# Down weights of a routed expert as two neighbouring rows for each partition, hidden features split into even and odd

## The reference

```
D_MODEL, SEQ, N_EXPERTS, TOP_K, EXPERT_DIM = 1024, 512, 64, 8, 256

def swiglu(t, wg, wu, wd):
    return (jax.nn.silu(t @ wg) * (t @ wu)) @ wd

# moe_ffn: every token goes to 8 of 64 experts, chosen by sigmoid scores
#   w_e_gate, w_e_up: (64, 1024, 256)      w_e_down: (64, 256, 1024)
    yb = swiglu(xb, w_e_gate[e], w_e_up[e], w_e_down[e])
    return yb * wb[:, None]
    ...
shared = swiglu(t, w_sh_gate, w_sh_up, w_sh_down)     # one expert for all tokens
```

## Time and profile before

| | us |
|---|---|
| median of three runs | 1057.78 |
| lowest, highest | 1054.84, 1062.67 |
| the profiled execution | 1054.87 |
| its span | 1053.1 |
| TensorE busy in it | 963.8 (92%) |
| VectorE, ScalarE, GpSimd busy | 547.2, 374.0, 506.1 |
| DMA | 295.13 MB, 280 GB/s over the span |

### The profile page before, as it was taken

The page is one execution under the profiler, slowest core; times in us unless marked ns, Lnnn a source line. Parts: engine busy times, 40 slices in busy tenths (PEclk is TensorE's granted clock), DMA queues, the critical chain, the costliest instruction groups (busy, mean ns, idle before and its releaser), DMA issues.

```text
span 1053.1 us, 19585 instructions
## 1 busy us (share of the span) xinstructions
PE 963.8 (92%) x5619; PEld 506.1 (48%) x5620; DVE 547.2 (52%) x835; ACT 374.0 (36%) x821; POOL 506.1 (48%) x349
## 2 busy tenths in 40 slices
PE   3999999899999998989999897999899999999870
PEld 0644444466455554545555454555455555555430
DVE  2336876876267833435545443454455455555335
ACT  4212221476345422323333332333233333333322
POOL 0313332000000035757777675677687777777650
PEclk9999999999999999999999998999999999999985
DMA  9955553700003948999998999999999999999816
GB/s 369 351 170 199 185 199 107 299 1 1 1 40 122 417 172 332 390 395 375 366 355 293 397 393 385 376 357 361 355 374 369 355 362 332 379 375 352 296 14 239
DMA packets 78025, 295.13 MB, mean 280 GB/s; under 512 B 18389, under 2 KB 19105, under 8 KB 58289
## 3 DMA queue, kind: packets, MB, share of 16 engines
q1 hardware_dynamic: 50450, 258.01, 62.6%
q0 software_dynamic: 26128, 34.65, 14.1%
q10 hardware_dynamic: 1424, 2.18, 0.6%
HBM read 280.83 MB, written 36.44 MB: 301 GB/s over the span
## 4 chain that ended last, share of the span: by engine, by line
PE 53%; DMA 34%; issue 4%; DVE 3%; ACT 2%; SPq 2%; POOL 1%; ACTq 1%; DVEq 0%; POOLq 0%
DMA wring<-in_w_e_down 26%; PE psum L1124 13%; PE psum L888 13%; PE psum L1133 6%; DMA xg<-h_rows,gidx 4%; PE psum L978 3%; PE psum L1090 3%; PE psum L958 3%; PE psum L925 3%; PE psum L949 2%; DMA ring<-in_w_ada 2%; SPq L429 1%; PE psum L1067 1%; PE psum L1112 1%; PE psum L1140 1%
## 5 line engine op out<-in xcount | busy, mean ns | idle before, releaser
L1124 PE MATMUL psum<-wring,rows 128*64 x1664 | 391.4, 389 | 0.7
L1124 PE MATMUL psum<-cur_g,rows 128*64 128x256 f32 x1664 | 391.5, 390 | 0.0
L515 POOL DMA_INDIRECT xg<-h_rows,gidx x214 | 274.8, 1284 | 164.7 <-issue 102.0
L1124 PEld LDWEIGHTS psum<-wring,rows 128*64 128x64 f32 x1664 | 223.9, 139 | 123.8 <-issue 13.6
L1124 PEld LDWEIGHTS psum<-cur_g,rows 128*64 128x64 f32 x1664 | 223.8, 139 | 0.0
L1538 DVE COPY cur_g<-wring 128x2048 f32 x105 | 131.2, 1250 | 146.4 <-issue 81.3
L522 POOL DMA_INDIRECT expert_sums<-rows,sidx x107 | 178.6, 1669 | 59.5 <-issue 33.9
L1133 PE MATMUL psum<-wring,rows 128*64 x420 | 199.0, 596 | 6.6 <-issue 4.2
L1133 PE MATMUL psum<-cur_d,rows 128*64 128x512 f32 x420 | 199.0, 596 | 0.0
L749 ACT COPY cur_d<-wring 128x1024 f32 x104 | 108.7, 1046 | 172.9 <-PE psum L1133 137.5
L1542 DVE STREAM_TRANSPOSE rows<-xg 128x512 f32<-128x512 f32 x105 | 116.3, 1108 | 57.7 <-DMA xg<-h_rows,gidx 57.2
(11 more groups left out here) (227 smaller groups left out, 934.2 us busy)
## 6 DMA issues: line engine op xcount, KB each, us to landing
wring<-in_w_e_gate SPq DMA_DIRECT2D x64, 1024.0 KB, 9.1
wring<-in_w_e_up SPq DMA_DIRECT2D x64, 1024.0 KB, 12.7
wring<-in_w_e_down SPq DMA_DIRECT2D x64, 1024.0 KB, 19.7
ring<-in_w_ada SPq DMA_DIRECT2D x20, 1024.0 KB, 5.1
ring<-in_w_in SPq DMA_DIRECT2D x4, 2048.0 KB, 28.6
heads<-in_w_ada SPq DMA_DIRECT2D x4, 1024.0 KB, 23.2
ring<-in_w_out SPq DMA_DIRECT2D x1, 4096.0 KB, 15.0
acc<-expert_sums SPq DMA_DIRECT2D x8, 512.0 KB, 7.2
```

The costliest lines, as they stand in the source:

```text
L515: pool.indirect_dma_start(xg[:, q, 256 * s:256 * s + 256], None, hrows, bass.IndirectOffsetOnAxis(gidx[:, q, s:s + 1].bitcast(U32), 0), bo ...
L1124: last = pe.matmul(pp[2][SUB * g:SUB * g + SUB, 512 * q:512 * q + 2 * P] .rearrange("p (u f) -> p u f", u=2), xT[:, q, k, :], cur_g[:, q, ...
```

## The change

The transfer of a routed expert's down weights takes two neighbouring rows for each partition: partition p now holds rows 2p and 2p+1, 8 KB in one piece. The shared expert's stay as they were. To match, hidden feature 2c goes to column c of group 0 and feature 2c+1 to column c of group 1: group 0's moving operand and VectorE's copy read every second word of gate and up. Number and order of the instructions stay the same on every engine, and so do their sizes.

```diff
                 else:
                     srcs = (a["w_e_gate"][0, n - 1].rearrange("(p k) f -> p (k f)", k=KD),
                             a["w_e_up"][0, n - 1].rearrange("(p k) f -> p (k f)", k=KD),
-                            a["w_e_down"][0, n - 1].rearrange("(j p) n -> p j n", j=FJ))
+                            a["w_e_down"][0, n - 1].rearrange("(p j) n -> p (j n)", j=FJ))
                 for s, src in enumerate(srcs):
                     o = (n % NB) * EW + s * CW
                     dst = wring[:, o:o + CW]
-                    if s == 2:
+                    if s == 2 and n == 0:
                         dst = dst.rearrange("p (j n) -> p j n", j=FJ)
                     sp.dma_start(dst, src).then_inc(s_wl[n % NB], 16)
...
             def gate_up(q, w0):
-                w = wring[:, bass.ds(w0, 2 * CW)].rearrange("p (u k f) -> p u k f", u=2, k=KD)
+                w = wring[:, bass.ds(w0, 2 * CW)].rearrange("p (u k f g) -> p u k f g", u=2, k=KD, g=2)
                 for k in range(KD):
                     for g in range(2):
                         last = pe.matmul(pp[2][SUB * g:SUB * g + SUB, 512 * q:512 * q + 2 * P]
                                          .rearrange("p (u f) -> p u f", u=2),
-                                         xT[:, q, k, :], cur_g[:, q, :, k, :] if g else w[:, :, k, 0:P],
+                                         xT[:, q, k, :], cur_g[:, q, :, k, :] if g else w[:, :, k, :, 0],
                                          start=(k == 0), stop=(k == KD - 1))
...
                 w0 = dve.snap(((e + 1) % NB) * EW)
-                w = wring[:, bass.ds(w0, 2 * CW)].rearrange("p (u k f) -> p u k f", u=2, k=KD)
+                w = wring[:, bass.ds(w0, 2 * CW)].rearrange("p (u k f g) -> p u k f g", u=2, k=KD, g=2)
                 dve.wait_ge(s_sh_st[1 + q], 16)
-                dve.tensor_copy(cur_g[:, q], w[:, :, :, P:]).then_inc(s_cgu, 1)
+                dve.tensor_copy(cur_g[:, q], w[:, :, :, :, 1]).then_inc(s_cgu, 1)
```

## The result

The change makes the kernel slower by 0.4%: 1063.52 us median of 18 runs (1058.12 to 1068.18) against 1059.02 of 18 runs before (1053.89 to 1062.67), ratio 1.0044 with a 95% interval of 1.0031 to 1.0058. Two more measurements on other chips gave 1.0036 (1.0017 to 1.0055) and 1.0046 (1.0026 to 1.0067). Within 1%, as forecast, but on the other side: I had forecast 1054 us. The profiled execution took 1062.6 us.

The account below looks back on a forecast made before the run. DMA engines and TensorE, both nearly full, were taken to bound the loop together. Transfers saved 2.2 us and both reads cost 0: 1054.87 - 2.2 = 1052.7 us, as a median forecast at 1054 us, range 1044 to 1078.

Parts of the forecast that it names:

- What bounds the kernel: In the loop over blocks, DMA engines and TensorE are both nearly full; neither alone can be called the bound.
- the 42 us on top of the blocks: Loop of 622 us against 580 for 104 blocks of 5.58: some 42 us of TensorE waiting, mostly for weights.
- Transfers, -2.2 us: Down loads in 8 KB pieces save 0.07 us each; on the 31 loads of the chain, 2.2 us faster.
- TensorE, "I take 0": In `gate_up`, 16 instructions a block reading every second word cost nothing: step near a plain run, reader slow.
- The far end of 3.9 us a block: Upper price of TensorE's read in `gate_up`, from `ada_rows` with columns eight words apart: 408 us in all, 1463 us.
- VectorE, 0: VectorE's copy of every second word stays at 1250 ns: price 0, with less confidence; other end 0.80 us.
- Rival A: VectorE's copy gets up to 0.80 us a block longer, delaying gathers and `hmid`: 1067 or 1089 us; chance 0.15.
- Rival B: TensorE reads slower in `gate_up`, 0.39 us a block, 41 us, part hidden by late weights: 1076 us; chance 0.08.
- Rival C: Longer pieces in the weight queue hold up gathers, 0.57 us a block later: 1066 us; chance 0.07.
- Rival D: Weight queue, served longer at each turn, gets late weights sooner, 5.4 us on 31 loads: 1047 us; chance 0.10.
- Rival E: Down pieces go out as 4 KB after all and nothing changes: 1055 us; chance 0.02.

## Why the prediction was wrong

- **What bounds the kernel**: held in the main. Two near-equal bounds lie side by side, and the 42 us on top of the blocks took in most of what the change added. But I called all 42 waiting, and only 27.2 were; most of the other 15 are work at the lower clock after long waits.
- **Transfers, -2.2 us**: the packets fell as worked out. The engine time fell by about 4 to 8 us, where I had 4.5 for all 64 loads. The time did not fall: 1.0008 and 1.0002. The first interval begins at 0.9989, a gain of 1.2 us at most; the second begins at 0.9978 and just lets 2.2 us through, so the term is not borne out and not excluded either. I took the DMA engines' time for the kernel's wherever a down transfer stood in the chain.
- **TensorE, "I take 0"**: this is the step that failed. The cost is 0.22 us a block and 23 us on the engine. In the full kernel the three runs with this read and the old transfers lost 1.2, 1.9 and 3.7 us by their ratios, the whole change 4.5. The far end of 3.9 us a block was nearly right for steps of four: blocks took 3.80 us more. I dismissed it as a whole because a step of two is "far nearer to a plain run". A plain column costs 0.84 ns and one at the far end 0.84 + 0.96 = 1.80; had I taken half of the latter for a step of two, 0.90 ns, it would have passed the plain pace of 0.84 by about what was measured. The row needed for it was there. The rule of the Trainium skill that I quoted ("SBUF — State Buffer", section "Specifications (TRN2)": lines of 16 bytes, and at least two hits in each for full bandwidth) is not quite what the runs show for TensorE: at two reads a line it is 7% slower (0.230 for 0.216 us). The prediction names another section of that page for it.
- **VectorE, 0**: held, 1242 to 1263 ns for 1250. The rule that spoke against it (the Trainium skill, "Vector Engine (DVE) Microarchitecture Reference", section 5.2: full rate only for runs of at least two adjacent words) does not hold for this copy.
- **Rival A** did not happen. **Rival B** did, at 6% of the far end, where I had asked for a tenth; of its 41 us I let half be hidden, and of the real 23 four fifths were. **Rival C**: rows are later the longer the weights' pieces are, and TensorE then waits more often (36 and 31 times for 14); but the kernel with the transfer alone is not slower, so at most this took back what the longer pieces saved. **Rival D**: no gain shows. **Rival E**: no, the packets fell by 8192.

That the time stayed within 1% and inside the range is in part luck: the price that I had put at nothing was 23 us on the engine, and the waits beside it kept four fifths of that from the end.

## What to carry to other kernels

Before TensorE is made to read an operand with a step, find how many fetches of 16 bytes a column takes and set that against the pace of the matmul. Here a fetch came to about 1.78 ns and a float32 column to 0.84: a quarter of a fetch a column (a plain run) hides behind that pace, and half a fetch (every second word) just passes it and is paid on every instruction. When two bounds lie side by side, a saving on one and a price on the other are not of one weight: ask for each how much of the waiting it fills or frees. Pieces of a large stream set how long small transfers wait behind it, which is worth watching in the waits: here it cost at most what the longer pieces saved.

## What the runs showed that I had not expected

- Steps of four words cost TensorE just as much as steps of eight (0.96 ns a column more). Two column groups, one slow and one plain, do not start together any more: at steps of two the plain one keeps its 0.216 us and gets at most one instruction ahead. At steps of four it starts its first six within about 1.2 us, and from then on two every 0.91 us, the pace of the slow group: it gets ahead by three and is then held.
- After an idle stretch of 4.26 us TensorE's granted clock fell to 0.50, and the block behind it took 7.36 us for 5.58. So 42 us of lost time in the loop held only 27.2 us of waiting.
- An issue on SyncE of 64 bytes ahead of each load costs 0.31%, 3 us in all.
- A deeper queue of loads helps from two to three experts (0.9968 and 0.9974) and not from three to four (1.0021). With four, SyncE tells the others late of weights that have arrived; whether that is all of it is open.
